# Routing tables on four column groups, logits formed turned on two column halves, and another order for the last tile's route

## The reference

```python
def hier_moe(h, w_rg, b_rg, w_re, b_re, w_gate, w_up, w_down):
    ...
    lg = (t @ w_rg).astype(jnp.float32) + b_rg.astype(jnp.float32)
    pg = jax.nn.softmax(lg, axis=-1)
    gsel = jnp.argmax(lg, axis=-1)
    pg_sel = jnp.take_along_axis(pg, gsel[:, None], axis=-1)
    le = ((t @ w_re).astype(jnp.float32) + b_re.astype(jnp.float32)).reshape(-1, N_GROUPS, EXPERTS_PER_GROUP)
    le_sel = jnp.take_along_axis(le, gsel[:, None, None], axis=1)[:, 0]
    top_v, top_i = lax.top_k(le_sel, TOP_K)
    gate = jax.nn.softmax(top_v, axis=-1) * pg_sel
    eidx = gsel[:, None] * EXPERTS_PER_GROUP + top_i
    comb = jnp.einsum('tk,tke->te', gate, jax.nn.one_hot(eidx, N_EXPERTS, dtype=jnp.float32))
    a = jnp.einsum('td,edf->tef', t, w_gate)
    b = jnp.einsum('td,edf->tef', t, w_up)
    act = jax.nn.silu(a) * b * comb[:, :, None].astype(t.dtype)
    y = jnp.einsum('tef,efd->td', act, w_down)
    return y.reshape(shp)
```

## Time and profile before

| | us |
|---|---|
| median of 3 runs | 1309.81 (1308.11 to 1310.07) |
| the profiled execution | 1307.46 |
| its span | 1305.6 |
| TensorE busy | 1193.0 (91%) |
| VectorE busy | 703.1 (54%) |
| ScalarE busy | 318.1 (24%) |
| GpSimd busy | 143.2 (11%) |
| mean granted TensorE clock | 0.956 of full |

### The profile page before, as it was taken

The page is one execution under the profiler, slowest core; times in us unless marked ns, Lnnn a source line. Parts: engine busy times, 40 slices in busy tenths (PEclk is TensorE's granted clock), DMA queues, the critical chain, the costliest instruction groups (busy, mean ns, idle before and its releaser), DMA issues.

```text
span 1305.6 us, 17526 instructions
## 1 busy us (share of the span) xinstructions
PE 1193.0 (91%) x6401; PEld 614.0 (47%) x6401; DVE 703.1 (54%) x2179; ACT 318.1 (24%) x916; POOL 143.2 (11%) x159
## 2 busy tenths in 40 slices
PE   7989979999999997888999999999867999999895
PEld 3435545555555545453555665555532334333231
DVE  1218889999999998331345544554552254212121
ACT  1133445345345356221111111121100110110000
POOL 0000000000000001100000000000001233333342
PEclk9998889999999998898999999999877999999898
DMA  8861000300000004257111011000666998999993
GB/s 323 304 239 27 1 1 25 151 12 33 33 1 33 25 1 167 97 208 286 33 48 49 1 49 48 33 5 28 280 245 237 403 337 310 320 380 385 389 358 63
DMA packets 48913, 194.88 MB, mean 149 GB/s; under 512 B 12240, under 2 KB 15094, under 8 KB 36515
## 3 DMA queue, kind: packets, MB, share of 16 engines
q1 hardware_dynamic: 37883, 173.79, 34.2%
q0 software_dynamic: 10368, 17.87, 5.7%
q10 hardware_dynamic: 576, 2.10, 0.4%
HBM read 172.60 MB, written 42.36 MB: 165 GB/s over the span
## 4 chain that ended last, share of the span: by engine, by line
PE 61%; DVE 24%; ACT 5%; DMA 4%; issue 4%; SPq 1%; POOL 0%; POOLq 0%; ACTq 0%; DVEq 0%
PE bank L830 12%; DVE W L1841 12%; PE bank L1350 10%; PE bank L1296 9%; PE bank L1357 6%; PE bank L1099 3%; PE bank L1274 3%; PE bank L1234 2%; PE bank L907 2%; PE bank L836 2%; DMA W<-in_w_exp_down 2%; PE bank L1339 2%; DVE W L1891 1%; DVE G L1785 1%; PE bank L1314 1%
## 5 line engine op out<-in xcount | busy, mean ns | idle before, releaser
L830 PE MATMUL bank<-W,G 128*128 128x512 f32 (+1 forms) x768 | 311.2, 561 | 3.8 <-DVE G L1785 3.0
L1841 DVE SCALAR_TENSOR_TENSOR W<-W,dwT 128x128 f32<-128x128 f32 (+1 forms) x1048 | 271.7, 336 | 0.0
L830 PEld LDWEIGHTS bank<-W,G 128*128 128x128 f32 x768 | 144.1, 191 | 148.8 <-issue 145.4
L1350 PE MATMUL bank<-W 128*32 128x512 f32 x1344 | 174.7, 604 | 1.7 <-DVE W L2337 1.7
L1099 PE MATMUL bank<-W 128*128 128x512 f32 x256 | 114.8, 608 | 3.9 <-issue 3.9
L1296 PE MATMUL bank<-W 128*128 128x512 f32 x256 | 113.3, 595 | 0.2 <-DVE W L2209 0.2
L703 POOL TENSOR_SCALAR st<-st 128x1 f32<-128x1 f32 (+3 forms) x40 | 8.0, 199 | 899.7 <-DVE st L1939 442.5
L2337 DVE TENSOR_TENSOR W<-bank,cvec 128x512 f32<-128x512 f32 x48 | 31.0, 686 | 139.2 <-PE bank L1339 139.2
L1350 PEld LDWEIGHTS bank<-W 128*32 128x32 f32 x1344 | 49.6, 112 | 108.5 <-issue 106.2
L1357 PE MATMUL bank<-W 128*32 128x512 f32 x672 | 87.3, 595 | 2.4 <-DMA W<-in_w_exp_down 1.4
L1099 PEld LDWEIGHTS bank<-W 128*128 128x128 f32 x256 | 49.1, 194 | 63.9 <-issue 63.6
(11 more groups left out here) (351 smaller groups left out, 1586.7 us busy)
## 6 DMA issues: line engine op xcount, KB each, us to landing
W<-in_w_exp_gate SPq DMA_DIRECT2D x27, 1024.0 KB, 13.0
W<-in_w_exp_up SPq DMA_DIRECT2D x27, 1024.0 KB, 15.4
W<-in_w_exp_down SPq DMA_DIRECT2D x27, 1024.0 KB, 18.3
W<-in_cache_mem_k SPq DMA_DIRECT2D x8, 1024.0 KB, 5.0
W<-in_cache_mem_v SPq DMA_DIRECT2D x8, 1024.0 KB, 7.2
W<-in_w_in SPq DMA_DIRECT2D x4, 1792.0 KB, 24.6
G<-in_w_exp_gate SPq DMA_DIRECT2D x5, 1024.0 KB
G<-in_w_exp_up SPq DMA_DIRECT2D x5, 1024.0 KB
```

The source lines that it names most:

```text
L830: mm = pe.matmul(bank[0:rows, at:at + hi - lo], HT[:, c, 0:rows], w[:, c, lo:hi], start=(c == 0), stop=(c == DC - 1))
L1350: mm = pe.matmul(B[2 + par][lo:hi, :], HG[par][:, c, lo:hi], WGU[u][:, :, c, :], start=(c == 0), stop=(c == DC - 1), skip_group_check=True)
L1841: dve.scalar_tensor_tensor(y, src, w, y, ALU.mult, ALU.add).then_inc(M["conv_tap"], 1)
```

## The change

- **Tables.** The table has 128 rows instead of 64: two choices x tokens, and two choices x gates, each of 32 rows. `table_part` makes them as four products of 32 columns, each on its own column group of the array, instead of two products of 64 that accumulate. `place` takes 64 rows, which adds the two choices. For the last tile first the tokens' two, later the gates' two.
- **Router.** The product is turned: 36 weight columns are stationary and H3's 128 tokens move; even chunks go to partitions 0 to 35, odd ones to 64 to 99. ScalarE copies both to `LT`, and one product with `PAIR` (`router_turn`) adds the halves and turns the logits back. It stands before the fourth chunk of `output_half(1)`. ScalarE's copies stand ahead of the `Square` of the next tile.
- **route_hot.** The selected group's eight logits come from a product and a reduction instead of four operations; two others (`- top`, the difference of the two best) go behind `r_hot`, with a semaphore of their own for `gate_exp`.
- **route_rows** is split: the gates' part is `route_shares`, in the last two passes behind H3 or behind the first indices. The product with `ones` goes ahead of the one with `tri` and of the wait for `r_hot`.
- **End.** z3's first transposes go to bank 1; the router may start on H3's first half; block 0's index is copied by itself and its gather starts on it; block 0's `gate_up` may start on the first half of its rows.

```diff
-            pool.wait_ge(M["route_ready"], 1)
             pool.wait_ge(M["z3_out"], 16 * NT)
             for n in range(2):
+                pool.wait_ge(M["route_ready"], n + 1)
                 gather(idx_i[:, BLOCKS[n]:BLOCKS[n] + 1], zg_in[n], ZG[n])
...
             def route_rank(s4):
 
                 n4 = rows_of(s4)
+                if s4:
+                    pe.wait_ge(M["r_acc"], AFTER["r_acc"] + s4)
+                    pe.matmul(B[3][:, 0:NE], ones, RA, start=True, stop=False)
                 pe.wait_ge(M["r_hot"], AFTER["r_hot"] + s4 + 1)
-                mm = pe.matmul(B[3][0:n4, 0:NE], tri[0:n4, 0:n4], RM[0:n4, :], start=True, stop=(s4 == 0))
-                if s4:
-                    mm = pe.matmul(B[3][:, 0:NE], ones, RA, start=False, stop=True)
-                mm.then_inc(M["r_rank"], 1)
+                pe.matmul(B[3][0:n4, 0:NE], tri[0:n4, 0:n4], RM[0:n4, :], start=(s4 == 0), stop=True).then_inc(M["r_rank"], 1)
+
+            def table_part(bank, c, n4):
+
+                for k in range(2):
+                    lo = 64 * c + NE * k
+                    mm = pe.matmul(bank[lo:lo + NE, 64:64 + POS], RQ[0:n4, k, c, :], RR[0:n4, k, :], start=True, stop=True, skip_group_check=True)
+                return mm
 
             def route_table(s4):
 
@@ -1150,13 +1162,31 @@
                 pe.wait_ge(M["r_rows"], AFTER["r_rows"] + s4 + 1)
                 if s4 < NT - 1:
                     pe.wait_ge(M["r_gates"], s4 + 1)
-                cols = 2 if s4 < NT - 1 else 1
                 if s4 == SORT_TILE:
                     pe.wait_ge(M["r_part"], AFTER["r_part"] + 1)
                     pe.matmul(B[3][:, 320:320 + NE], ones, RA, start=True, stop=True)
-                for k in range(2):
-                    mm = pe.matmul(B[3][0:cols * NE, 64:64 + POS], RQ[0:n4, k, 0:cols, :].rearrange("p c e -> p (c e)"), RR[0:n4, k, :], start=(k == 0), stop=(k == 1))
+                mm = table_part(B[3], 0, n4)
+                if s4 < NT - 1:
+                    mm = table_part(B[3], 1, n4)
                 mm.then_inc(M["r_table"], 1)
+
+            def router(s3):
+
+                n3 = rows_of(s3)
+                wr = view(WR, 0, DC, 36)
+                pe.wait_ge(M["wr_in"], 32)
+                for c in range(DC):
+                    if c % 4 == 0:
+                        pe.wait_ge(M["h3_ready"], AFTER["h3_ready"] + 2 * s3 + c // 4 + 1)
+                    lo = 64 * (c % 2)
+                    mm = pe.matmul(B[1][lo:lo + 36, 0:n3], wr[:, c, :], H3[:, c, 0:n3], start=(c < 2), stop=(c >= DC - 2), skip_group_check=True)
+                mm.then_inc(M["rt_done"], 1)
+
+            def router_turn(s3):
+
+                n3 = rows_of(s3)
+                pe.wait_ge(M["lt_ready"], AFTER["lt_ready"] + s3 + 1)
+                pe.matmul(B[1][0:n3, 256:292], LT[0:100, 0:n3], PAIR[0:100, :], start=True, stop=True).then_inc(M["rtt_done"], 1)
...
-                rows = slice(lo, lo + NE)
+                rows = slice(lo, lo + 2 * NE)
...
+                table_part(B[6], 1, 128).then_inc(M["r_gtable"], 1)
...
-                            mm = pe.transpose(B[half][:, c * 128:c * 128 + n3], Z3[0:n3, k * 128:(k + 1) * 128], ident[0:n3, 0:n3])
+                            mm = pe.transpose(B[1 - half][:, c * 128:c * 128 + n3], Z3[0:n3, k * 128:(k + 1) * 128], ident[0:n3, 0:n3])
                         mm.then_inc(M["z3t_done"], 1)
-                    if s3 == NT - 1:
-                        route_table(s4)
-                def output_half(half):
+                def output_half(half, turned=-1):
                     for c in range(DC):
+                        if c == 3 and turned >= 0:
+                            router_turn(turned)
                         mm = pe.matmul(B[2 + half][0:n2, :], OT2[:, c, 0:n2], w_mo[:, c, 512 * half:512 * half + 512], start=(c == 0), stop=(c == DC - 1))
                     mm.then_inc(M["mo_done"], 1)
...
-                    pe.wait_ge(M["h3_ready"], AFTER["h3_ready"] + 2 * s3 + 2)
-                    pe.wait_ge(M["wr_in"], 32)
-                    wr = view(WR, 0, DC, 36)
-                    for c in range(DC):
-                        mm = pe.matmul(B[1][0:n3, 0:36], H3[:, c, 0:n3], wr[:, c, :], start=(c == 0), stop=(c == DC - 1))
-                    mm.then_inc(M["rt_done"], 1)
+                    router(s3)
                 if 0 < s2 < NT:
                     if s4 >= 0:
                         pe.wait_ge(M["r_acc"], AFTER["r_acc"] + s4 + 1)
-                    output_half(1)
+                    output_half(1, s3)
+                elif s3 == NT - 1:
+                    route_table(s4)
+                    router_turn(s3)
...
+            def gate_up(tiles, par, upper=0):
                 for c in range(DC):
+                    if c == DC // 2 and upper:
+                        pe.wait_ge(M["hg_ready"], upper)
...
+                act.wait_ge(M["r_odds"], AFTER["r_odds"] + s4 + 1)
...
+                if 0 <= s3 < NT:
+                    n3 = rows_of(s3)
+                    act.wait_ge(M["rt_done"], AFTER["rt_done"] + s3 + 1)
+                    act.activation(LT[0:36, 0:n3], B[1][0:36, 0:n3], ACT.Copy)
+                    act.activation(LT[64:100, 0:n3], B[1][64:100, 0:n3], ACT.Copy).then_inc(M["lt_ready"], 1)
                 if 2 <= s1 + 1 < NT:
...
+                    link(dve.memset(TABLE[2 * NE:4 * NE, :], 0.0))
...
-                link(dve.tensor_scalar(lg[:, 0:NG], lg[:, 0:NG], top[:, 0:1], None, ALU.subtract))
-                link(dve.tensor_scalar(sel, lg[:, NG:NG + EPG], og[:, 0:1], None, ALU.mult))
-                for g in range(1, NG):
-                    link(dve.scalar_tensor_tensor(sel, lg[:, NG + EPG * g:NG + EPG * g + EPG], og[:, g:g + 1], sel, ALU.mult, ALU.add))
+                own = RP3[0:n, 0, :]
+                link(dve.tensor_tensor(own.rearrange("p (g e) -> p g e", g=NG), lg[:, NG:36].rearrange("p (g e) -> p g e", g=NG), bc(og, EPG, 2), ALU.mult))
+                link(dve.tensor_reduce(sel, own.rearrange("p (g e) -> p e g", g=NG), X, ALU.add))
                 first_max(T_O[0:n, 0, :], sel, top[:, 1:2], EPG)
                 link(dve.scalar_tensor_tensor(sel, T_O[0:n, 0, :], -3e38, sel, ALU.mult, ALU.add))
                 first_max(T_O[0:n, 1, :], sel, top[:, 2:3], EPG)
                 for k in range(2):
                     link(dve.tensor_tensor(RO[0:n, k, :].rearrange("p (g e) -> p g e", g=NG), bc(og, EPG, 2), bc(T_O[0:n, k, :], NG, 1), ALU.mult))
-                link(dve.tensor_tensor(lg[:, 4:5], top[:, 2:3], top[:, 1:2], ALU.subtract))
                 dve.tensor_tensor(RM[0:n, :], RO[0:n, 0, :], RO[0:n, 1, :], ALU.add).then_inc(M["r_hot"], 1)
+                link(dve.tensor_scalar(lg[:, 0:NG], lg[:, 0:NG], top[:, 0:1], None, ALU.subtract))
+                dve.tensor_tensor(lg[:, 4:5], top[:, 2:3], top[:, 1:2], ALU.subtract).then_inc(M["r_odds"], 1)
...
             def route_rows(s4):
 
                 n = rows_of(s4)
-                keep, gate = LG[0:n, 36 * s4 + 5:36 * s4 + 9], LG[0:n, 36 * s4 + 9:36 * s4 + 11]
-                part = T_GATE[0:n, :]
+                keep = LG[0:n, 36 * s4 + 5:36 * s4 + 9]
                 link(dve.tensor_scalar(RQ[0:n, :, 0, :], RO[0:n], tok[0:n, s4:s4 + 1], None, ALU.mult))
                 dve.wait_ge(M["r_rank"], AFTER["r_rank"] + s4 + 1)
                 link(dve.tensor_tensor(RP3[0:n], RO[0:n], bc(B[3][0:n, 0:NE], 2, 1), ALU.mult))
                 link(dve.tensor_reduce(keep[:, 0:2], RP3[0:n], X, ALU.add))
                 link(dve.tensor_scalar(RR[0:n, 0, :], iota[0:n, :], keep[:, 0:1], None, ALU.is_equal))
                 dve.tensor_scalar(RR[0:n, 1, :], iota[0:n, :], keep[:, 1:2], None, ALU.is_equal).then_inc(M["r_rows"], 1)
-                dve.wait_ge(M["r_exp"], AFTER["r_exp"] + s4 + 1)
-                link(dve.tensor_scalar(part[:, 2:3], part[:, 1:2], 1.0, part[:, 0:1], ALU.add, ALU.mult))
-                link(dve.reciprocal(gate[:, 0:1], part[:, 2:3]))
-                link(dve.tensor_tensor(gate[:, 1:2], gate[:, 0:1], part[:, 1:2], ALU.mult))
-                link(dve.tensor_scalar(RQ[0:n, 0, 1, :], RO[0:n, 0, :], gate[:, 0:1], None, ALU.mult))
-                dve.tensor_scalar(RQ[0:n, 1, 1, :], RO[0:n, 1, :], gate[:, 1:2], None, ALU.mult).then_inc(M["r_gates"], 1)
+
+            def route_shares(s4):
+
+                n = rows_of(s4)
+                keep, gate = LG[0:n, 36 * s4 + 5:36 * s4 + 9], LG[0:n, 36 * s4 + 9:36 * s4 + 11]
+                part = T_GATE[0:n, :]
                 a = dve.tensor_tensor(RA[0:n, :], RA[0:n, :], RM[0:n, :], ALU.add)
                 if s4 == NT - 1:
                     a.then_inc(M["r_tot"], 1)
@@ -2074,6 +2107,12 @@
                     dve.wait_ge(M["r_part"], AFTER["r_part"] + 1)
                 else:
                     link(a)
+                dve.wait_ge(M["r_exp"], AFTER["r_exp"] + s4 + 1)
+                link(dve.tensor_scalar(part[:, 2:3], part[:, 1:2], 1.0, part[:, 0:1], ALU.add, ALU.mult))
```

(58 more changed lines are left out.)

13 lines of the change are left out of this document (7 added, 6 removed).

## The result

The changed kernel takes 1315.59 us, the median of five runs (1313.47 to 1321.61), beside 1308.12 for the kernel before in the same session (1307.85 to 1310.07, five runs). The ratio is 1.0057, 95% interval 1.0042 to 1.0072: **7.5 us slower**. The forecast was 15 to 17 slower. The sign and the wait behind it are as forecast, the size is about half.

What follows compares the result with a forecast made beforehand. TensorE's issue plus its stops bounds the loop; the last route is serial. 7.0 + 3.4 - 0.7 - 6.5 + 0.2 = +3.4 us, plus 12.5 for the clock, +15.9: 1325 us, range 1310 to 1335.

Steps and rivals of the forecast that it cites:

- a pass, 3 to 7: Steady passes with a router and a next tile to normalise: each 1.4 us longer, +7.0 us in all.
- pass 2: Pass that routes tile 0, with 64 rows and no tables: projection later after the router's start, +3.4 us.
- passes 8 and 9: Passes with no next `Square`, where logits wait only for the turn: -0.7 us together.
- last route: Serial routing of the last tile, from last adds to first `gate_up`: -6.5 us, bounds -7.2 and -4.
- the clock: TensorE's idle before the projection lowers its clock at five of six boundaries, 2.5 us each: +12.5, bounds 0 and 17.4.
- The wait that comes in: `LT` copies wait for `rt_done` ahead of the next tile's `Square`, delaying `norm_z`, logits, adds and projection; +1.4 us a steady pass.
- R': Router's start in a pass of the changed kernel, forecast 0.5 us earlier than in the kernel before.
- Tables, router, turn: TensorE work per pass: tables 1.01 to 0.5 us, router 1.70 to 0.85, turn adds 0.21; about 1.1 saved.
- The first: Rival: order costs as forecast but 2.9 us of idle doesn't lower the clock: +3.4, some 1313 us; chance 0.16.
- The fourth: Rival: the delay is real, few boundaries lower the clock, and it ends within 0.2%; chance 0.06.
- Column groups that don't overlap: Rival: no overlap in router and tables, so the router is out 0.85 us later: +8.3, some 1334; chance 0.08.
- Lateness that is covered: Rival: the `Square`'s lateness is hidden if `rt_done` to `norm_z` takes 1 us: -12, some 1298; chance 0.10.

Runs made afterwards that it cites:

- experiment 3: Changed kernel plus three unused products on TensorE where it would stand before the projection, passes 3 to 8: 1315.73 us, ratio 1.0051.
- Experiment 2: Kernel before, with only one wait added: ScalarE's `Square` of the next tile waits for `rt_done`: 1334.91 us, ratio 1.0198; profiled again: 1334.47.
- experiment 1: Changed kernel with ScalarE's two `LT` copies moved behind the next tile's `Square`: 1305.06 us, ratio 0.9958 to the kernel before.
- Experiments 6 and 7: Each on experiment 4: `route_shares` back behind `route_rows` in passes 10 and 11, 1296.23 us; both gathers wait for all indices, 1299.77 us.
- the first repeat: Changed kernel run again unedited, one profile, first of three: 1317.42 us, beside 1308.84 for the kernel before.
- experiment 4: Changed kernel with `Square` ahead of the `LT` copies and the turn two chunks earlier in `output_half`: 1296.12 us, ratio 0.9897 to the kernel before.

## Why the prediction was right in sign and wrong in size

| term | forecast | measured |
|---|---|---|
| router's start to `norm_z` | 3.55 | 3.85 |
| to the logits | 5.5 | 5.7 |
| to the first add | 10.1 | 10.25 |
| to the projection | 12.8 | 12.87 |
| a pass, 3 to 7 | +1.4 | +1.6 (pass 6: +2.0) |
| pass 2 | +3.4 | +3.3 |
| passes 8 and 9 | -0.7 | +0.2 |
| last route | -6.5 | -6.1 |
| sum without the clock | +3.4 | +5.9 |
| the clock | +12.5, five falls of 2.5 | 4.3 to 4.6 in the profiles, two falls |

**The wait that comes in** was right to 0.3 us at each step. The router's start comes 0.35 us earlier than before instead of 0.5, the projection at R'+12.87 instead of 12.8; these two and the one pass of 44.60 make the 1.5 us by which passes 3 to 7 exceed their +7.0. Passes 8 and 9 give 0.9 more and the last route 0.4, while the 0.2 for the setup is not visible. The lengths without falls come from experiment 3's trace, passes 2 to 7; its timed +6.0 agrees with the 5.9, though its own trace has pass 9 1.5 us longer than the changed kernel's, at a lower clock in its first 19.3 us (0.65 against 0.73), so the agreement holds to a microsecond or two. Experiment 2 shows that the wait alone slows the kernel before, and experiment 1 that without it the changed kernel is faster than before.

**Tables, router, turn.** 0.57, 1.00 and 0.14 us against 0.5, 0.85 and 0.21 forecast. The router came out 0.15 longer than two halves at a time would give. The Trainium skill (TensorEngine Tiling (Array Packing), Key Properties) says a change of tiling mode drains TensorE, from which the prediction had worked out 0.16 to 0.3 less saved; the trace agrees with that in size, but no run here tells a drain from a slower product.

**The last route** saved 6.1 instead of 6.5 and kept it to the end, as forecast: the expert part took 313.1 against 312.8. Experiments 6 and 7 show 1.4 and 1.5 of it to be the later shares and the early first gather.

**The step that failed is "The clock", +12.5.** I took the 2.51 us of the earlier trace rows, saw that the clock was at half behind it, and concluded that five of six stops of 2.9 us would do the same, at 2.5 each. The stops came nearly as forecast (3.67 in pass 2 where the sum had 4.2, then 2.75 to 3.12 where it had 2.9). But only those of passes 2 and 3 lowered the clock, in four profiles of four, and the second cost 1.5 to 1.6. So the profiles have 4.3 to 4.6 us of clock where the sum had 12.5. The 2.5 was too high for a steady pass because it leaned on the 2.9 of the expert loop's row: there TensorE was busy 5.43 us at half clock (1213.8 to 1220.5), and behind the stop of pass 3 only 2.92. (The upper end of the forecast's own range was also set too high: six falls of 2.9 give 1330.6 and not 1332.)

How much of the timed +7.5 is the clock's stays uncertain. Less the 5.9 to 6.0 of the rest it is some 1.5, within the scatter. But behind the start, which moves from run to run, the four profiles of the changed kernel are 10.0 to 11.2 us longer than the one of before, and over all eight of its runs the median is 1318.1. The mean granted clock doesn't sort the runs: the five of the first session are 1313.47 (0.960), 1314.47 (0.961), 1315.59 (0.960), 1318.86 (0.956) and 1321.61 (0.956), and the first repeat, whose trace has both falls, has 0.960 too.

Open stays why passes 2 and 3 and not 4 to 7. It is not the length of the stop alone: 2.76 lowered the clock in pass 3 and 3.12 didn't in pass 6, and in experiment 2 equal stops of 3.22 did in three passes and not in two. In these repeats it wasn't chance from run to run either, nor the time since the start of the execution, which differed by up to 4.8 us.

**The rivals.** The first, order as forecast and no fall (1313), comes nearest in time, but its reason is wrong: the clock does fall. The fourth had the right condition, few boundaries that lower the clock (two of six), but its end within 0.2% didn't come (0.57% slower), since the rest alone costs 5.9 us. Column groups that don't overlap are refuted by 0.57 and 1.00 us. Lateness that is covered is refuted by the 2.76 us stop; but its condition, from `rt_done` to `norm_z` in 1 us, isn't needed once the `Square` stands first, and experiment 4 then gives 1296, close to the 1298 worked out for it. I had seen that only ScalarE's order stood in the way; where the turn stood, I had costed for passes 8 and 9 alone (logits at R'+3.9) and not for a mended order.
